# Ten of the 31 taps of a depthwise convolution tile move from VectorE to ScalarE and GpSimd

## The reference, cut to what matters

```
def causal_depthwise_conv(u, w):          # w: 31 x 256
    return conv(u, w, padding left 30, one filter per feature)

def conformer_conv(ab, w_dw, ln_g, ln_b, w_pw):
    a, b = split(ab, 2)
    u = a * sigmoid(b)
    u = causal_depthwise_conv(u, w_dw)    # out[t] = sum over k of w[k] * u[t - 30 + k]
    u = silu(layer_norm(u, ln_g, ln_b))
    return u @ w_pw
```

## Time and profile before

| | us |
|---|---|
| median of 3 runs (1512.19 to 1512.54) | 1512.44 |
| profiled execution | 1511.85 |
| its span | 1510.0 |
| PE busy | 1460.6 (97%) |
| DVE busy | 821.7 (54%) |
| ACT busy | 571.1 (38%) |
| POOL busy | 258.4 (17%) |

### The profile page before, as it was taken

One profiled execution on the slowest core, in us unless ns is written; L12 is line 12 of the kernel. 1 busy time (PEld: TensorE's weight loads), 2 busy tenths in 40 slices (PEclk: granted clock), 3 DMA queues, 4 the chain that ended last, 5 costly groups with the idle time before them and its releaser, 6 DMA issues.

```text
span 1510.0 us, 17740 instructions
## 1 busy us (share of the span) xinstructions
PE 1460.6 (97%) x6978; PEld 1189.7 (79%) x6978; DVE 821.7 (54%) x1151; ACT 571.1 (38%) x837; POOL 258.4 (17%) x170
## 2 busy tenths in 40 slices
PE   9989989999999999989999999999999999999998
PEld 7766768888888887766789877788887888888887
DVE  5598566433333346674767753634445665534554
ACT  5344534522323224543364565422224443323310
POOL 4244244300101013340034202200003000000000
PEclk9999999999999999998999999999999999999999
DMA  6221222333333332211211111232332233332331
GB/s 225 72 71 55 70 70 85 98 98 98 98 98 98 98 98 72 83 56 56 71 56 49 37 56 43 87 109 86 100 106 86 70 112 102 94 112 84 98 98 70
DMA packets 36131, 129.18 MB, mean 86 GB/s; under 512 B 4024, under 2 KB 4280, under 8 KB 36048
## 3 DMA queue, kind: packets, MB, share of 16 engines
q1 hardware_dynamic: 35760, 127.78, 27.5%
q10 hardware_dynamic: 288, 0.26, 0.1%
HBM read 125.91 MB, written 2.10 MB: 85 GB/s over the span
## 4 chain that ended last, share of the span: by engine, by line
PE 84%; DVE 8%; ACT 3%; POOL 2%; issue 2%; DMA 0%; ACTq 0%; DVEq 0%; POOLq 0%
PE P L1030 24%; PE P L1031 24%; PE P L1032 24%; PE P L1269 2%; PE P L1051 1%; DVE P L1825 1%; PE P L1052 1%; PE P L1053 1%; POOL AC L2304 1%; PE P L1155 1%; POOL H L2313 1%; ACT WH L1349 1%; DVE WL L1670 1%; POOL DD L2304 0%; PE P L1252 0%
## 5 line engine op out<-in xcount | busy, mean ns | idle before, releaser
L1030 PE MATMUL P<-AH,WH 128*128 128x512 f32 x1104 | 445.3, 403 | 16.6 <-issue 5.0
L1031 PE MATMUL P<-AL,WH 128*128 128x512 f32 x1104 | 433.8, 393 | 0.0
L1032 PE MATMUL P<-AH,WL 128*128 128x512 f32 x1104 | 433.8, 393 | 0.0
L1349 ACT ACTIVATE WH<-WR 128x1024 fp32r<-128x1024 f32 x232 | 243.9, 1052 | 327.3 <-PE P L1032 320.4
L1670 DVE TENSOR_TENSOR WL<-WR,WH 128x1024 fp32r<-128x1024 f32 x215 | 270.7, 1259 | 160.7 <-ACT WH L1349 160.3
L1030 PEld LDWEIGHTS P<-AH,WH 128*128 128x128 f32 x1104 | 209.7, 190 | 68.4 <-issue 16.9
L1032 PEld LDWEIGHTS P<-AH,WL 128*128 128x128 f32 x1104 | 209.5, 190 | 45.0
L1031 PEld LDWEIGHTS P<-AL,WH 128*128 128x128 f32 x1104 | 209.9, 190 | 42.0 <-issue 0.7
L1030 PE MATMUL P<-FH,WH 128*128 128x512 f32 x432 | 168.0, 389 | 0.0
L1031 PE MATMUL P<-FL,WH 128*128 128x512 f32 x432 | 168.0, 389 | 0.0
L1032 PE MATMUL P<-FH,WL 128*128 128x512 f32 x432 | 168.0, 389 | 0.0
(11 more groups left out here) (306 smaller groups left out, 1870.8 us busy)
## 6 DMA issues: line engine op xcount, KB each, us to landing
WR<-in_ws SPq DMA_DIRECT2D x232, 512.0 KB, 3.6
out<-Y SPq DMA_DIRECT2D x8, 256.0 KB, 2.0
H<-in_xT SPq DMA_DIRECT2D x3, 512.0 KB, 8.0
C<-in_const SPq DMA_DIRECT2D x1, 946.5 KB, 10.9
H<-in_xT SPq DMA_DIRECT2D x2, 256.0 KB, 4.5
PR<-in_pT SPq DMA_DIRECT2D x1, 512.0 KB, 4.5
WR<-in_ws SPq DMA_DIRECT2D x1, 384.0 KB, 4.8
WR<-in_ws ACTq DMA_DIRECT2D x1, 128.0 KB, 4.2
```

Source lines behind the costliest of these rows:

```text
L1030: e.matmul(P, wh, xh, start=start, stop=False)
L1031: e.matmul(P, wh, xl, start=False, stop=False)
L1032: ins = e.matmul(P, wl, xh, start=False, stop=stop)
L1349: e.activation(m.WH[:, c % NW, :], m.WR[:, c % NRAW, :], ACT.Copy).then_inc(*at.up("w_hi", "w_hi", c))
```

## The change

`SIDE = 10`. DVE starts each tile at tap 10 and adds 21 taps in PSUM. Taps 0 to 9 are side taps: ACT multiplies the shifted input by the weight of the tap (`side_tap` 0 writes `ACC`, 1 to 9 write the two halves of `SQ1` in turn), and POOL adds each product to `ACC`. ACT may be two side taps ahead of POOL. At the end DVE adds the PSUM sum to `ACC` (`side_sum`). A side tap is said with every second tap of DVE, and the layer-norm steps follow 30 blocks earlier than before. The squares of the later step `p1` also wait for the last side addition, as they use the same buffer.

```diff
+SIDE = 10
     def conformer(self):
         t = self.bank(6)
         for j in range(2):
-            for tap in range(31):
+            for tap in range(SIDE, 31):
                 self.say("dwconv", t, j, tap)
+                if (tap - SIDE) % 2 == 0 and (tap - SIDE) // 2 < SIDE:
+                    self.say("side_tap", j, (tap - SIDE) // 2)
                 yield 1 + tap % 2
+            self.say("side_sum", t, j)
# ScalarE, square
+        if n == "p1":
+            w.wait_ge(*at("side_add", 1, SIDE - 1))
# ScalarE
+    def side_tap(j, i):
+        u, k = m.UP[:, j, i:i + T], m.p("dw", 31 * j + i)
+        w.wait_ge(*at("glu", j))
+        if i == 0:
+            e.activation(m.ACC[:, j, :], u, ACT.Copy, scale=k).then_inc(*at.up("side_tap", "side_tap", j, i))
+            return
+        w.wait_ge(*at("summed", "1", 7))
+        if i >= 3:
+            w.wait_ge(*at("side_add", j, i - 2))
+        elif j:
+            w.wait_ge(*at("side_add", 0, SIDE - 1))
+        e.activation(m.SQ1[:, i % 2, :], u, ACT.Copy, scale=k).then_inc(*at.up("side_tap", "side_tap", j, i))
# VectorE, dwconv
-        if tap == 0:
+        if tap == SIDE:
             w.wait_ge(*at("glu", j))
             if j:
-                w.wait_ge(*at("conv1", 0, 30))
+                w.wait_ge(*at("conv1", 0))
             else:
                 w.wait_ge(*at("read", t.before.id))
-            e.tensor_scalar(P, u, k, None, ALU.mult).then_inc(*at.up("conv1", "conv1", j, tap))
+            e.tensor_scalar(P, u, k, None, ALU.mult).then_inc(*at.up("conv1", "tap", j, tap))
         else:
-            w.wait_ge(*at("conv1", j, tap - 1))
-            e.scalar_tensor_tensor(P if tap < 30 else m.ACC[:, j, :], u, k, P, ALU.mult, ALU.add).then_inc(
-                *at.up("conv1", "conv1", j, tap))
-        if tap == 30:
-            at.also(("conv1", j, tap), "conv1", j)
-            if j:
-                at.also(("conv1", j, tap), "read", t.id)
+            w.wait_ge(*at("tap", j, tap - 1))
+            e.scalar_tensor_tensor(P, u, k, P, ALU.mult, ALU.add).then_inc(*at.up("conv1", "tap", j, tap))
+
+    def side_sum(t, j):
+        a = m.ACC[:, j, :]
+        w.wait_ge(*at("tap", j, 30))
+        w.wait_ge(*at("side_add", j, SIDE - 1))
+        e.tensor_tensor(a, a, m.bank[t.bank][:], ALU.add).then_inc(*at.up("conv1", "conv1", j))
+        if j:
+            at.also(("conv1", j), "read", t.id)
# GpSimd
+    def side_tap(j, i):
+        if i == 0:
+            return
+        a = m.ACC[:, j, :]
+        w.wait_ge(*at("side_tap", j, i))
+        turn()
+        e.tensor_tensor(a, a, m.SQ1[:, i % 2, :], ALU.add).then_inc(*at.up("side_add", "side_add", j, i))
+        did("side_add", j, i)
```

More of the change, by code:

```diff
@@ L1646, in scalar_program @@
     run = {"load_first": load_first, "w_hi0": w_hi0, "w_hi": w_hi, "x_hi": x_hi, "square": square, "v1": v1, "forget1": forget1, "exp1": exp1, "scale1": scale1,
-           "turned1": turned1, "split1": split1, "glu_gate": glu_gate, "ln_center": ln_center, "ln_out": ln_out,
-           "pool_means": pool_means, "sc_b": sc_b, "mix1": mix1, "ple_in": ple_in, "up1": up1, "ple_proj": ple_proj,
+           "turned1": turned1, "split1": split1, "glu_gate": glu_gate, "side_tap": side_tap, "ln_center": ln_center,
+           "ln_out": ln_out, "pool_means": pool_means, "sc_b": sc_b, "mix1": mix1, "ple_in": ple_in, "up1": up1, "ple_proj": ple_proj,
            "ple_gate": ple_gate, "va_turn": va_turn, "decay1": decay1, "qk_square": qk_square, "qk_rows": qk_rows,
@@ L2262, in vector_program @@
            "forget_in": forget_in, "forget0": forget0, "forget2": forget2, "mask1": mask1, "scale1": scale1,
-           "split1": split1, "glu_gate": glu_gate, "glu": glu, "dwconv": dwconv, "ln_mean": ln_mean,
+           "split1": split1, "glu_gate": glu_gate, "glu": glu, "dwconv": dwconv, "side_sum": side_sum, "ln_mean": ln_mean,
            "ln_center": ln_center, "ln_var": ln_var, "ln_out": ln_out, "pool_in": pool_in, "pool_means": pool_means,
@@ L2439, in gpsimd_program @@
     run = {"w_lo_pool": w_lo_pool, "square": square, "residual": residual, "clear1": clear1, "glu_gate": glu_gate,
-           "pool_sums": pool_sums, "sc_c": sc_c, "sc_h": sc_h, "ple_in": ple_in, "up1": up1, "lv_clear": lv_clear,
+           "side_tap": side_tap, "pool_sums": pool_sums, "sc_c": sc_c, "sc_h": sc_h, "ple_in": ple_in, "up1": up1, "lv_clear": lv_clear,
            "lv_ref": lv_ref, "lv_scale": lv_scale, "st_scale0": st_scale0, "gn_square": gn_square, "gn_out": gn_out,
```

## The result

The changed kernel takes 1529.49 us (median of 4, 1525.48 to 1530.26) against 1512.32 us: a ratio of 1.0126, interval 1.0105 to 1.0147. Run again on another chip it gave 1.0128 (1.0102 to 1.0153). It is slower, as forecast, but by 17 us and not by 7.3, and outside the range by half a microsecond. The profiled execution took 1525.48 us, 13.6 more than that of before (1511.85); its span is 1523.7. It is the fastest of the four.

What follows compares the result with a forecast made beforehand. PE was taken as the bound, busy for 97% of the span, with 11 us to win. The terms 2.5 + 3 + 1 + 0.5 + 1.5 - 1.66 - 0.7 + 1.2 gave +7.3 us, 1519.7; range 1509 to 1529.

Steps and rivals of the forecast that it cites:

- DVE isn't relieved before block 62: Blocks 1 to 62: tap spacing is kept, DVE does 42 taps before and now; all relief comes after block 62.
- POOL's instructions get in between those of `pool_means`: Blocks 23 and 60: ready POOL work delays DVE's two-operand instructions; 2.5 us at `pool_means` 0, 3 at `pool_means` 1.
- `side_sum` 0: Block 32: DVE waits for the ninth side addition, with a `WL` ahead of it; 0 to 2 us, taken as 1.
- ACT's 0.5: A side tap issued ahead of the transposes' copy in its block makes PE wait; 0 to 3 us, taken as 0.5.
- The layer norm, 30 blocks earlier: Norm from block 63: `ln_mean` costs 1.5 us, while 1.66 and 0.7 of PE's waits are given back.
- The term for `ln_mean`: Block 63, behind `side_sum` 1: PE waits for DVE's backlog, a tap and the sum; 0 to 3 us, taken as 1.5.
- the 1.66: PE's wait of 1.66 us at 189.39, in the norm's tiles, goes because attention still fills PE; -1.66.
- The 0.7 that I gave back: Of PE's wait of 1.19 us at 153.74, 0.7 is won; least gain 0.
- The table load at 0: `ln_out`'s Silu between attention's exponentials needs one more 1.28 us load on ACT; costed at 0, without cover 1.3.
- Clock: If the wait at 92 grows from 1.2 to 4, another dip is likelier than not: 0 to 3.4 us, taken as 1.2.
- ACT held by POOL: Rival, chance 0.07: ACT's two `SQ1` slots are used up while POOL is busy, and PE waits too; +15, 1527.
- The relief is what counts: Rival, chance 0.17: taps ending earlier let DVE run ahead from 136 on; up to -6.7 us, likely -4, 1508.4.

Runs made afterwards that it cites:

- e2_no_side: Changed kernel with the side taps left out on ACT and POOL (taps 0 to 9 missing from the result), norm still early: 1520.77 us, 1.0074.
- e1_ln_late: Changed kernel with 30 blocks between `side_sum` 1 and `ln_mean`, so the norm is at block 93 as before; side work stays: 1517.02 us, 1.0049.
- e3_no_pool: Changed kernel with only POOL's 18 additions left out; ACT still multiplies: 1521.93 us, 1.0071.
- e6_apart: Changed kernel with taps over 46 blocks a tile, norm at block 93 and side taps placed away from `pool_means`; full result: 1507.60 us, 0.9993.
- e5_no_side_late: Changed kernel without side taps and with the norm 30 blocks later, at block 93 as before: 1508.95 us, 1.0001.
- e9_gap3: Changed kernel without side taps, `ln_mean` 3 blocks behind `side_sum` 1: 1519.72 us, 1.0074.
- e9_gap15: Changed kernel without side taps, `ln_mean` 15 blocks behind `side_sum` 1: 1510.15 us, 1.0008.
- e10_ln_low: Changed kernel without side taps, norm early, the two low parts of `ln_out` said 5 blocks after its multiplications: 1516.60 us, 1.0052.
- e7_no_side_spread: Changed kernel without side taps, its 21 taps a tile spread over 46 blocks, norm at block 93: 1508.06 us, 0.9994.
- e8_again: The changed kernel again, unchanged, for a second profile beside other kernels on one chip: 1528.63 us, 1.0128.

## Why the prediction was right in its sign and wrong in its size
- *DVE isn't relieved before block 62.* Right. e2_no_side has the wait of before at block 62, 1.56, with ten taps missing.
- *POOL's instructions get in between those of `pool_means`.* Right in mechanism, and in size too: 2.5 + 3 + 1 + 0.5 forecast, plus a share of the clock; e1_ln_late measures 0.49%, 7.4 us, for all of it. The waits near 92 and 136 grew by 2.6 and 2.4 us. Of its parts, `side_sum` 0 did wait 0.95 us on DVE (forecast 1), but no wait of PE follows; ACT's 0.5 is too small to be seen (e3_no_pool). So 1.5 us of these terms did not show on PE, the clock took more than its share, and that the total fits so closely is in part luck. What POOL adds to DVE there was shown by e6_apart, which moves it away.
- *"The layer norm, 30 blocks earlier": failed.* The prediction put +1.5 for `ln_mean` and gave back 1.66 and 0.7, a gain of 0.9 us. e2_no_side and e5_no_side_late measure 0.73%, 11 us, for this step. The term for `ln_mean` itself was a wait of 0.50 in the changed kernel and 1.39 without side work, inside its bounds of 0 to 3, and the 1.66 did go. The 0.7 that I gave back did not: the wait of 1.19 there became 2.58, with the steps of the variance ahead of it. What I left out is what the norm's steps do to what is queued behind them. The claim was that "attention still fills PE between `ln_out` and the two tiles". But attention needs DVE and ACT for each unit, and `ln_out` holds DVE in order for 6.5 us while it waits for PE and ACT; in e9_gap3 it holds ACT in the same way. PE did not fill `ln_out`'s gap with attention; `ln_out` stopped attention, and PE had 3.70 us of nothing. e9_gap15 and e10_ln_low bear this out, the second for a part.
- *The table load at 0: mis-sized, but small.* One more was needed, as forecast. The one for the Silu fell where ACT was idle; the one back for the last exponential stood ahead of a copy that PE waited for, 0.75 us in the changed kernel and 1.23 in e10_ln_low. "PE's need for it is blocks away" didn't hold. The next ACTIVATE starts 1.30 us after the load's start (174.06 to 175.36), as in the earlier trace rows.
- *Clock.* Named and mis-sized: 1.2 for one dip more near 92, which came (1.6). The dip that costs most follows the wait at block 62: before it lasted some 4 us, now 12, with the 16 single-column products of `ln_mean` in it, which took 3.57 us in place of 1.8 before. Behind block 62 PE is busy for 6.4 us more with the same work and idle for 4.7 more: over half of the 11 us there are the clock, and the prediction had no term for it at that place. Its "a wait of 2.01 us at 83 did not lower it" holds for the profile of before, e3_no_pool and e9_gap15 only: behind the same wait the clock of the next 4 us fell to 0.65 or 0.66 in e1_ln_late, e2_no_side and e9_gap3.
- *Rivals.* "ACT held by POOL" did not occur: each ACT side tap began right behind other ACT work, and nothing waited for an addition. That its 1527 is nearer to the measured time than the forecast is chance. "The relief is what counts" fell: e7_no_side_spread shows that there was at most 0.2% to be had.
- *Against the signs named:* taps x40 at 752 ns, POOL at 49.9 us, additions at 1302 ns on average, PE's wait near 92 at 3.79, a wait at L1170, all as said. `DD` grew to 1258 ns only; it was the 16-column instruction that took the wait, not its neighbour.

In e2_no_side's profile 5.5 of the 9.4 us behind block 62 are PE's slower work and 3.9 its idle time. What stays open is why the dip behind block 62 lasts 12 us. With the products of `ln_mean` right behind it, it cost 3.4 to 6.8 us in the five profiles that have them; without, 0 to 3.4 in the others, e9_gap3 and e9_gap15 included, whose waits there are those of before. So these products go with a longer dip, but no kernel here changes the clock alone, and the dips differ between executions of one program. The four times of e8_again run from 1523.02 to 1533.03 us.

## What to carry to other kernels
Before moving work from one engine to another, ask whether the plan spaces it by the clock or by counts: here the taps kept their spacing, so the work left where nobody waited. When something gets shorter, what follows it comes earlier, and a serial chain through several in-order queues belongs where nothing else needs these queues; moving one 30 blocks cost more than the side work. Here it wasn't the sum of POOL's load that hurt DVE but a POOL instruction ready beside a row of short DVE instructions with two SBUF operands; the same additions some blocks away cost nothing that can be seen.

## What the runs showed of the hardware
DVE's running sum over the forget gates (TENSOR_TENSOR_SCAN, 4 x 512) took 3.42 us before and 1.21 in the changed kernel. Before, POOL's `WL` had started 0.05 us ahead of it; DVE's row and POOL's row:

```profile
69.33 3.42 DVE L1766 TENSOR_TENSOR_SCAN FX<-FX 4x512 f32<-4x512 f32 x1
...
69.28 2.40 POOL L2294 TENSOR_TENSOR WL<-WR,WH 128x1024 fp32r<-128x1024 f32 x1 [0.53 <-ACT WH L1349]
```

It ended 1.07 us after POOL did, so it waited for the whole of it, as `DD` and `DL` do. In the changed kernel the `WL` came 1.6 us after the scan's start (68.77 against 67.14), and the 2.2 us were won by chance; the wait of 2.01 of the earlier trace rows at 83.22 is absent in that profile. The other profiles agree. In eight of the 13 the scan took 3.42 to 3.45 us, each time with a `WL` that had started 0.01 to 0.06 us ahead of it; in five it took 1.21, with POOL's next instruction 1.6 us or more behind its start. Both happen with and without side work, so a comparison of two single profiles holds these 2.2 us as chance.

In `pool_means` a DVE instruction of 16 columns, 0.17 us by itself, took 2.25 us beside a `WL`.
